# Low part of streamed weights: an accumulating DMA onto the negated rounded weights in place of a GpSimd subtraction

## The reference

```python
def swiglu(h, w_gate_up, w_down):            # layers 1 and 2, D_FF = 2816
    gate, up = jnp.split(h @ w_gate_up, 2, axis=-1)
    return (jax.nn.silu(gate) * up) @ w_down

def squared_relu_mlp(h, w_up, w_down):       # layer 3, D_FF_2 = 4096
    return jnp.square(jax.nn.relu(h @ w_up)) @ w_down
...
x = x + swiglu(rmsnorm(x, norm_ffn[i]), ffn_w_gate_up[i], ffn_w_down[i]).astype(x.dtype)
```

## Time and profile before

| | us |
|---|---|
| median of 2 runs | 1847.69 |
| lowest, highest | 1847.45, 1847.93 |
| span of the profiled execution, first to last instruction | 1845.6 |

### The profile page before, as it was taken

The page is one execution under the profiler, slowest core; times in us unless marked ns, Lnnn a source line. Parts: engine busy times, 40 slices in busy tenths (PEclk is TensorE's granted clock), DMA queues, the critical chain, the costliest instruction groups (busy, mean ns, idle before and its releaser), DMA issues.

```text
span 1845.6 us, 24588 instructions
## 1 busy us (share of the span) xinstructions
PE 1807.7 (98%) x9676; PEld 1453.6 (79%) x9676; DVE 1139.4 (62%) x1671; ACT 832.7 (45%) x1351; POOL 732.3 (40%) x430
## 2 busy tenths in 40 slices
PE   7999999999999999999999999999999999999998
PEld 5778888888887688678888888887776768888886
DVE  8952337546475698853365474732536558787878
ACT  6752523333344436765333233453467464343434
POOL 1223343444333477443434434243245443324222
PEclk9999999999999999999999999999999999999999
DMA  5454351440502222004423314125210233415041
GB/s 192 100 137 109 120 153 52 128 124 23 160 23 75 72 90 91 24 24 136 138 69 114 116 45 137 46 87 160 60 57 24 81 98 108 135 49 173 10 137 46
DMA packets 195534, 171.82 MB, mean 93 GB/s; under 512 B 15914, under 2 KB 169002, under 8 KB 195034
## 3 DMA queue, kind: packets, MB, share of 16 engines
q1 hardware_dynamic: 193122, 166.45, 30.2%
q10 hardware_dynamic: 2296, 3.78, 0.6%
HBM read 163.10 MB, written 2.65 MB: 90 GB/s over the span
## 4 chain that ended last, share of the span: by engine, by line
PE 91%; DVE 4%; ACT 2%; issue 1%; POOL 1%; DMA 0%; POOLq 0%; DVEq 0%; ACTq 0%
PE PS L2659 79%; PE PS L3021 2%; PE PS L3012 2%; PE PS L3031 2%; PE PS L2528 1%; DVE taken L2365 1%; PE PS L2571 1%; PE PS L2971 1%; PE PS L2938 0%; ACT probs_t L1462 0%; PE PS L2520 0%; PE PS L2586 0%; PE PS L2580 0%; ACT sq_junk L1119 0%; PE PS L2732 0%
## 5 line engine op out<-in xcount | busy, mean ns | idle before, releaser
L786 POOL TENSOR_TENSOR w_lo<-raw,w_hi 128x2048 fp32r<-128x2048 f32 x92 | 430.0, 4674 | 604.2 <-ACT w_hi L1064 582.6
L2659 PE MATMUL PS<-xT_hi,w_hi 128*128 128x512 f32 (+1 forms) x1160 | 444.2, 383 | 3.1 <-DVE xT_lo L1894 2.0
L2659 PE MATMUL PS<-xT_lo,w_hi 128*128 128x512 f32 (+1 forms) x1160 | 441.4, 380 | 0.0
L2659 PE MATMUL PS<-xT_hi,w_lo 128*128 128x512 f32 (+1 forms) x1160 | 441.2, 380 | 0.0
L1064 ACT ACTIVATE w_hi<-raw 128x2048 fp32r<-128x2048 f32 x105 | 201.3, 1917 | 332.5 <-PE PS L2659 325.0
L2659 PEld LDWEIGHTS PS<-xT_hi,w_hi 128*128 128x128 f32 x1160 | 217.7, 188 | 49.9 <-issue 8.6
L2659 PEld LDWEIGHTS PS<-xT_lo,w_hi 128*128 128x128 f32 x1160 | 217.7, 188 | 42.2
L2659 PEld LDWEIGHTS PS<-xT_hi,w_lo 128*128 128x128 f32 x1160 | 217.8, 188 | 41.3
L793 POOL TENSOR_TENSOR w_lo<-dn_raw,w_hi 128x1024 fp32r<-128x1024 f32 (+1 forms) x46 | 123.4, 2704 | 262.5 <-ACT w_hi L1230 262.5
L2659 PE MATMUL PS<-w_hi,xT_hi 128*128 128x512 f32 (+1 forms) x560 | 219.9, 393 | 1.5 <-issue 1.5
L2659 PE MATMUL PS<-w_hi,xT_lo 128*128 128x512 f32 (+1 forms) x560 | 216.5, 387 | 0.0
(11 more groups left out here) (411 smaller groups left out, 2757.0 us busy)
## 6 DMA issues: line engine op xcount, KB each, us to landing
raw<-in_ffn_w_gate_up SPq DMA_DIRECT2D x88, 512.0 KB, 5.1
dn_raw<-in_ffn_w_down SPq DMA_DIRECT2D x22, 1024.0 KB, 7.7
raw<-in_w_up SPq DMA_DIRECT2D x32, 512.0 KB, 5.5
dn_raw<-in_w_down SPq DMA_DIRECT2D x16, 1024.0 KB, 7.6
raw<-in_dsa_w_in SPq DMA_DIRECT2D x28, 512.0 KB, 4.3
raw<-in_w_in SPq DMA_DIRECT2D x21, 512.0 KB, 5.0
raw<-in_s_w_glu SPq DMA_DIRECT2D x32, 256.0 KB, 4.9
raw<-in_dsa_w_o SPq DMA_DIRECT2D x8, 512.0 KB, 4.1
```

The lines of the kernel that those rows point to most:

```text
L786: pool.tensor_tensor(w_lo[:, g % 2, :], raw[:, r % 2, :], f32(w_hi[:, g % 2, :]), ALU.subtract).then_inc(w_split, 1)
L2659: ins = mm(o, a if weights_stay else c, c if weights_stay else a, start=first and n == 0, stop=last and n == 2, skip_group_check=onto)
```

## The change

In 47 up slots (SUM_SLOTS: those that `up_splits` handed to `split_run`) the low part is made in another way. ScalarE first writes the negated rounded weights into w_lo (the rounding is that of the fp32r output, scale -1), signals w_minus, and then writes w_hi as before. GpSimd waits for w_minus and issues a DMA from raw to w_lo that adds to what is there: w_lo = raw - round(raw). It waits until that has landed and until w_hi is there, and then sets one element column of a new tile `summed` by a memset, whose completion gives w_split the same increment as before.

```diff
+SUM_SLOTS = [up_slot(g0, j, run, dns) for g0, run, dns, ups in ((FFN_SLOT[0], FFN_RUN, FFN_DN, FT), (FFN_SLOT[1], FFN_RUN, FFN_DN, FT),
+                                                               (MLP_SLOT, MLP_RUN, MLP_DN, MLP_UP))
+             for j in range(2, ups) if not (j % run == 1 and 1 <= j // run <= dns)]
...
+        summed = fixed("summed", [P, len(SUM_SLOTS)])
...
+        w_minus, w_sum = sem("w_minus"), sem("w_sum")
...
+            def split_sum(g):
+
+                r, n = raw_of(g), SUM_SLOTS.index(g) + 1
+                pool.wait_ge(w_minus, n)
+                if g - 1 in SPLIT_DVE:
+                    pool.wait_ge(w_split, r)
+                pool.dma_start(w_lo[:, g % 2, :], raw[:, r % 2, :], accum_op=ALU.add).then_inc(w_sum, 16)
+                pool.wait_ge(w_sum, 16 * n)
+                pool.wait_ge(w_rounded, r + 1)
+                pool.memset(summed[:, n - 1:n], 0.0).then_inc(w_split, 1)
+
...
                     else:
-                        split_run(up_slot(g0, j, run, dns), 1)
+                        split_sum(up_slot(g0, j, run, dns))
...
                 if g >= 2:
                     act.wait_ge(w_used, g - 1)
+                if g in SUM_SLOTS:
+                    act.activation(w_lo[:, g % 2, :], raw[:, r % 2, :], ACT.Copy, scale=-1.0).then_inc(w_minus, 1)
                 act.activation(w_hi[:, g % 2, :], raw[:, r % 2, :], ACT.Copy).then_inc(w_rounded, 1)
```

## The result

| | before | after |
|---|---|---|
| median, us | 1847.69 | 1904.64 |
| lowest, highest | 1847.45, 1847.93 | 1904.42, 1904.86 |
| span of the profiled execution | 1845.6 | 1902.8 |

The change makes the kernel slower: 1.0307 times the time before, interval 1.0277 to 1.0337, 57 us. The forecast was 1897 us in a range of 1846 to 2010.

The account below looks back on a forecast made before the run. The prediction took TensorE, busy 98% of the 1845.6 us span, as the bound. It added 27 late slots of 1.8 us, 49 us, for a span of 1894.6 us and a forecast of 1897 us, range 1846 to 2010.

Parts of the forecast that it names:

- The bound: Feed-forward parts are unbroken TensorE matmuls, TensorE 98% busy; relieving GpSimd or VectorE is worth 0.
- ScalarE's rounding, price 0: 47 added roundings of 1.92 us on ScalarE, 90 us in all, hidden within the up slots.
- The budget, 8.63 us: Time from GpSimd's start in an up slot until TensorE needs the low part.
- D alone, 8.3 us: Accumulating transfer from issue through memset, DMA engines otherwise idle: 8.1 us from x_res's memory-read row plus 0.2.
- The sharing, 2.0 and 4.6 us: Overlap with loads, without or with a down load, shared evenly, delays the transfer to 10.3 or 12.9 us at most.
- How lateness adds up: With two w_lo buffers every other slot pays: 27 payments of 1.8 us, 49 us.
- the hidden case: Rival: the transfer stays under 8.6 us in nearly all up slots, so no change, 1846 to 1884 us; chance 0.37.
- The signs: Landing time under 8.4 us means hidden, 10 to 12 the forecast, over 13 serial; wrong if ScalarE waits for raw.
- the price of 0 for the loads: Raw loads issued after w_split land in 5.1 us, leaving over 4 us before ScalarE rounds, so they cost nothing.
- The much slower transfer: Rival: adder or software descriptors set the transfer's pace, 14 to 18 us each, 1999 to 2186 us; chance 0.24.
- GpSimd's own pace: GpSimd makes one transfer at a time, so a slot lasts at least transfer plus 0.1 us; limiting from 12.9 us.
- The rule of the Trainium skill on descriptors held up by VectorE: GpSimd's descriptor writing stalls while VectorE is in a two-port mode, slowing the transfer; chance 3 in 100.

Follow-up runs that it names:

- e3b_copy_sliver: e2_all_sliver with the transfer a plain copy of raw onto w_lo that adds nothing; 1847.8 us in a single run.
- e4_act_only: Kernel before plus only ScalarE's added negated rounding into w_lo; GpSimd subtracts as before, no accumulating DMA; 1848.4 us, ratio 1.0005.
- e1_down_sliver: Changed kernel with down loads of all chunks but the first of each part cut from 1 MB to 64 KB; 1866.8 us, ratio 1.0101.
- e10_spread: Changed kernel with down loads of the first two chunks of the first two parts issued in every other slot; 1922.1 us, ratio 1.0401.
- e8_late_3us: Kernel before, no accumulating DMA, with GpSimd given 7.1 us more work in ten slots; 1896.7 us, ratio 1.0263.
- e2_all_sliver: e1_down_sliver with the up slots' raw loads also cut from 1 MB to 128 KB a slot; 1849.9 us in a single run.

## Why the prediction was right

*The bound.* That nothing could be won was right: VectorE's hs_lo fell from 4.53 to 0.69 us and GpSimd lost 177 us of work, and no microsecond of it appeared. e3b_copy_sliver, with the same relief and no wait, ends at the time of before and not under it.

*ScalarE's rounding, price 0.* Measured in e4_act_only: 0.05%, inside the interval.

*The budget, 8.63 us.* About 8.4 us by e1_down_sliver.

*D alone, 8.3 us.* Measured 7.1 us, so the row of x_res was 1.2 us too long. To count two reads was right all the same: the copy takes 4.3 us, and the engine time doubles.

*The sharing, 2.0 and 4.6 us.* This term was mis-sized in both directions, and "shared evenly" was the wrong step. What counts is how far ahead the loads were issued. Behind raw loads issued 2.6 us or more ahead, D is mostly 7.1 to 8.2 us, so 0 to 1.1 us. Beside raw loads issued together with the transfer, as happens behind a late slot, it is up to 11.2 us with no down load at all. Beside a down load it is mostly 9 to 13 us, so 2 to 6 us. The sum of both terms, 12.9 us at most, was right by compensation; 13.1 us is the largest in the trace, and that transfer has two down loads beside it.

*How lateness adds up.* That every other late slot pays is in the trace for large waits (none of the ten over 2 us is followed by another in the next slot; e10_spread shows the price of breaking up neighbours). Small ones do come in a row: 1.1 and 0.4 us, 0.6 and 0.7 us, and 1.2, 1.4 and 0.4 us in neighbouring slots. The count was too high: 27 payments forecast, 19 found, since light slots don't pay at all. The size was 1.8 us forecast and 2.0 found. The 1.8 us was a choice between 0 and 4.3 us, and not quite the number it was said to be: the lower overlap of 2.0 us gives a lateness of 1.7 us. 49 us forecast, 38.2 found.

*What was missing.* The slow stretch behind a wait, 12.7 us and some 2 us at the starts. The prediction priced a stall at its length. e8_late_3us puts a wait of 3.2 us at 4.7 to 4.9 us. The total of 57 us agrees with 49 only because this term came in where the count was too high. So the path and the kind of loss were forecast, at 0.38 against 0.37 for the hidden case; that the sum came so near is luck.

*The signs.* The landing time, 9.3 us in the median, lies between the hidden case (under 8.4) and the forecast (10 to 12). The prediction would call itself wrong if ScalarE waited for raw. It did, in three places, 14.7 us in all; the price of 0 for the loads, with over 4 us left, doesn't hold where a raw load takes 11 us.

*The rivals.* Hidden was wrong with the loads as they are, though D was under the budget in 16 of 47 slots and TensorE waited in only 19. The much slower transfer never came up. GpSimd's own pace did: nine transfers were issued the moment the one before had landed, but TensorE waited behind none of them. The rule of the Trainium skill on descriptors held up by VectorE ("SBUF — State Buffer", Who interferes with whom) had 3 in 100; with VectorE's tensor_tensor instructions beside it, D alone stayed at 7.1 us in e2_all_sliver in most slots, so nothing here shows it.

## What to carry to other kernels

Before work is moved from an idle engine to the DMA engines, sum their time within one slot (here 3.9 us of raw loads and 3.0 of a down load, from the shares of 11 us in the earlier trace rows, and 5.2 of an accumulating transfer, twice a copy's, in 10.88 us). Then look at the order of issue: a transfer issued behind others starts when they are nearly through. Where TensorE has no gap, a faster engine beside it is worth nothing, and a new gap costs more than its length: 3.2 us of wait cost 4.8 us. With two buffers, late slots that are neighbours share one payment; here bursts of load were cheaper together than spread out, by 17 us.

## What the runs showed of the hardware

- GpSimd's accumulating DMA of 1024 KB from SBUF to SBUF: 0.87 us to issue, 7.0 us to land, 5.2 us of 16 engines. The plain copy: 0.54 us, 4.2 us, 2.7 us.
- Beside loads issued ahead of it by SyncE it loses more than an even share: a copy of 2.7 us of engine time lost up to 6.3 us. The first packet of the accumulating transfer starts 1.4 us after the issue with the engines free, up to 5.0 us after it behind loads.
- Packet for packet the engines alternate between such a transfer (8 KB) and raw loads (512 B): 98 and 97 packets in 4 us, 196 and 12 KB a microsecond. The raw loads then take up to 11.5 us to land.
- After TensorE had stood for 3.0 to 3.5 us, its granted clock was at half for 3.4 us (6.8 us once) in eight of ten cases; after 1.3 to 1.9 us in two of ten. Why some waits pass without it is open.
